# Merge gates of a hybrid encoder as seven products per block, with both branch projections ahead of them

## The reference, cut to what matters

```python
h = rms_norm(x, norm_g[layer])
z = h @ w_in[layer]
qa, ka, va, ga, qr, kr, vr, gr, gm = split_columns(z)
ya = (silu(ga) * attention(qa, ka, va)) @ w_branch_attn[layer]      # 512 -> 1024
yb = (silu(gr) * group_norm(retention(qr, kr, vr))) @ w_branch_ret[layer]   # 512 -> 1024
gates = sigmoid(gm).reshape(b, s, 2, d)                             # gm: 2048 columns of z
merged = gates[:, :, 0] * ya + gates[:, :, 1] * yb
x = x + merged @ w_out[layer]
```

## Time and profile before

| | |
|---|---|
| median of 3 runs | 1902.31 us |
| profiled execution | 1906.54 us |
| its span | 1904.7 us |
| TensorE matmuls | busy 1809.2 us, 95% of the span, x10784 |
| VectorE | busy 1062.2 us, 56% |
| ScalarE | busy 664.9 us, 35% |
| GpSimd | busy 696.1 us, 37% |
| DMA traffic | 96.09 MB, mean 50 GB/s |

### The profile page before, as it was taken

One profiled execution on the slowest core, in us unless ns is written; L12 is line 12 of the kernel. 1 busy time (PEld: TensorE's weight loads), 2 busy tenths in 40 slices (PEclk: granted clock), 3 DMA queues, 4 the chain that ended last, 5 costly groups with the idle time before them and its releaser, 6 DMA issues.

```text
span 1904.7 us, 30067 instructions
## 1 busy us (share of the span) xinstructions
PE 1809.2 (95%) x10784; PEld 1594.2 (84%) x10784; DVE 1062.2 (56%) x2378; ACT 664.9 (35%) x1551; POOL 696.1 (37%) x581
## 2 busy tenths in 40 slices
PE   6899989999999999999899998999999999999996
PEld 5788968899999888887687888889999988888875
...
DMA packets 129736, 96.09 MB, mean 50 GB/s; under 512 B 15712, under 2 KB 114272, under 8 KB 129632
## 3 DMA queue, kind: packets, MB, share of 16 engines
q1 hardware_dynamic: 127232, 89.42, 14.9%
...
## 4 chain that ended last, share of the span: by engine, by line
PE 74%; DVE 14%; POOL 4%; issue 4%; ACT 2%; DMA 1%; POOLq 0%; SPq 0%; DVEq 0%; ACTq 0%
PE ps L602 18%; PE ps L604 18%; PE ps L603 18%; PE ps L738 4%; PE ps L727 4%; DVE xh L1825 3%; PE ps L751 2%; PE ps L753 2%; POOL pp L483 2%; PE ps L844 2%; PE ps L828 1%; DVE lsum L1803 1%; DVE us L1678 1%; DVE hT_lo L1812 1%; PE ps L698 1%
## 5 line engine op out<-in xcount | busy, mean ns | idle before, releaser
L602 PE MATMUL ps<-w_hi,hT_hi 128*128 128x256 f32 (+1 forms) x1280 | 391.9, 306 | 12.8 <-DVE hT_lo L1436 4.9
L604 PE MATMUL ps<-w_hi,hT_lo 128*128 128x256 f32 (+1 forms) x1280 | 377.7, 295 | 0.0
L603 PE MATMUL ps<-w_lo,hT_hi 128*128 128x256 f32 (+1 forms) x1280 | 377.6, 295 | 0.0
L429 POOL TENSOR_SCALAR w_hi<-raw 128x1024 fp32r<-128x1024 f32 x97 | 102.8, 1060 | 558.2 <-PE ps L604 523.7
L602 PEld LDWEIGHTS ps<-w_hi,hT_hi 128*128 128x128 f32 x1280 | 245.7, 192 | 17.7 <-DVE hT_lo L1436 6.6
L602 PE MATMUL ps<-hT_hi,w_hi 128*128 128x512 f32 x640 | 255.2, 399 | 0.0
L604 PE MATMUL ps<-hT_hi,w_lo 128*128 128x512 f32 x640 | 252.2, 394 | 0.0
L603 PE MATMUL ps<-hT_lo,w_hi 128*128 128x512 f32 x640 | 252.0, 394 | 0.0
L603 PEld LDWEIGHTS ps<-w_lo,hT_hi 128*128 128x128 f32 x1280 | 245.9, 192 | 0.3
L604 PEld LDWEIGHTS ps<-w_hi,hT_lo 128*128 128x128 f32 x1280 | 245.5, 192 | 0.0
L483 POOL TENSOR_SCALAR pp<-pp,rrc 128x1024 f32<-128x1024 f32 x128 | 143.9, 1124 | 166.5 <-DVE rrc L1595 159.2
...
## 6 DMA issues: line engine op xcount, KB each, us to landing
raw<-w_in SPq DMA_DIRECT2D x167, 256.0 KB, 3.3
...
xh<-xs SPq DMA_DIRECT2D x8, 1024.0 KB, 9.6
raw<-w_a SPq DMA_DIRECT2D x16, 256.0 KB, 2.8
raw<-w_r SPq DMA_DIRECT2D x16, 256.0 KB, 3.2
w<-w_o SPq DMA_DIRECT2D x4, 1024.0 KB, 10.3
...
xh<-x SPq DMA_DIRECT2D x2, 1024.0 KB, 9.2
```

The lines of the kernel that those rows point to most:

```text
L429: nc.gpsimd.tensor_scalar(place(pos)[0], raw[:, slot], 1.0, 1.0, ALU.mult, ALU.mult).then_inc(w_rounded, 1)
L602: nc.tensor.matmul(outp, ah, bh, start=(start and i == 0), stop=False)
L603: nc.tensor.matmul(outp, ah, bl, start=False, stop=False)
L604: last = nc.tensor.matmul(outp, al, bh, start=False, stop=(stop and i == len(pairs) - 1))
```

## The change

The stage of gates and branches is rewritten, in both layers.

- Both branches come first: 16 groups of branch A, then 16 of branch B, 12 matmuls each, weights in 8 units of two blocks. ScalarE copies A's results to `y_st`, from which SyncE writes them to DRAM (`ys`); B's go to `xm`. The last head's crosses stand behind groups 0 and 1 of A, its turn-outs behind group 4.
- The gates of one block m are a 2 x 2 by 2 x 2 block product (token halves and channel halves of h; channel halves and kinds A/B of the weights), made as seven products of 12 matmuls each. VectorE makes four sums of quarters of h once per layer (`sum_3`, `sum_1`, `sum_2`, `sum_4`), which ScalarE and VectorE split into high and low parts; they lie in `ua_hi`, `ua_lo`, `ur_hi` and in place of a quarter of hT.
- Weights of the gates: GpSimd makes four sums or differences per block (`g_total`), ScalarE all seven high parts (`g_hi_part`), VectorE all seven low parts (`g_lo`). They run one block ahead, in eight slots.
- Product results: ScalarE copies the first (`g_first`), VectorE adds or subtracts the others (`give`) into four gate tiles in `w1x`; ScalarE takes tanh (`g_tanh`), VectorE merges with the branches (`merge_a` reads ya back from DRAM by way of `hb`, `merge_b`, `merge_sum`).
- The loops over m are written out, and the drain and wait on `phase_end` ahead of the stage are gone. The first O stage steps on VectorE and ScalarE stand between the additions of the last block, and SyncE's loads for the O stage hang on other events.

```diff
+N_Q = 7
+GIVES = ((((0, 0), None, 1),), (((0, 1), (0, 0), 1),), (((0, 0), (0, 0), 1),), (((1, 0), (0, 1), 1),),
+         (((1, 1), (1, 0), 1), ((0, 1), (0, 1), 1)), (((1, 0), (1, 0), -1),), (((0, 1), (0, 1), 1),))
+GIVEN = [0, 1, 2, 3, 5, 6, 7]
+N_GIVE = GIVEN[-1]
+TANHS = ((0, 0), (1, 1), (1, 0), (0, 1))
+HI_AT = (0, 2, 1, 3, 4, 5, 6)
+LO_DVE, LO_POOL = (0, 2, 1, 3, 4, 5, 6), ()
+N_S = 4
+E_OPS = 20
+E_DONE = {3: 6, 1: 12, 2: 16, 4: 20}
...
+        def g_slot(t_, x):
+            e = x % 8
+            return t_[:, 4 * (e % 2):4 * (e % 2) + 4, e // 2 * P:(e // 2 + 1) * P]
...
+                def spill(g):
+                    sp.wait_ge(y_ev, L * N_G + g + 1)
+                    sp.dma_start(ys[g // 2 * P:(g // 2 + 1) * P, g % 2 * 512:(g % 2 + 1) * 512], y_st[:, g % 2]).then_inc(y_out[g % 2], 16)
+                def gate_raw(m, b):
+                    mm = L * K + m
+                    if m:
+                        sp.wait_ge(*lo_done(mm - 1, (4, 3, 5, 6)[b]))
+                        if b == 0:
+                            sp.wait_ge(g_sum, 4 * mm)
+                    elif b < 2:
+                        sp.wait_ge(w_ready, 1 + u0 + U_A + K - 1 + b)
...
+                for v in range(6):
+                    branch_unit(v)
+                for g in range(N_G):
+                    spill(g)
+                    if g in (4, 9):
+                        branch_unit(6 + (g == 9))
+                for b in (0, 2, 1, 3):
+                    gate_raw(0, b)
+                y_back(0)
+                y_back(1)
...
-                sp.wait_ge(x_saved, L * 16 + 16)
-                sp.dma_start(w12[:], block(0, 1)).then_inc(o_w12a, 16)
-                sp.wait_ge(w_ready, 1 + L * U_L + U_L)
+                for m in range(1, K):
+                    for b in (1, 0, 2, 3):
+                        gate_raw(m, b)
+                    if m >= 2:
+                        y_back(m)
+                    if m == 1:
+                        sp.wait_ge(e_lo, (L + 1) * 2 * N_S)
+                        sp.dma_start(w12[:], block(0, 1)).then_inc(o_w12a, 16)
+                for q in (4, 6):
+                    sp.wait_ge(*lo_done((L + 1) * K - 1, q))
+                sp.wait_ge(g_sum, (L + 1) * K * 4)
                 sp.dma_start(w22, block(1, 1)).then_inc(o_w22, 16)
-                wait_apart(sp, d_ya, L * (2 * K) + 2 * K)
-                x_block(1, 1)
+                x7 = ((L + 1) * K - 1) * N_Q
+                sp.wait_ge(g_p, x7 + 2)
                 x_block(0, 1)
-                wait_apart(sp, d_yb, L * (2 * K) + 2 * K)
+                sp.wait_ge(d_mg, (L + 1) * N_G - 2)
                 for h in range(2):
                     sp.dma_start(w11[:, 2 * h:2 * h + 2], block(0, 0, 2 * h, 2)).then_inc(o_w11[h], 16)
+                sp.wait_ge(g_p, x7 + 4)
+                x_block(1, 1)
+                x_block(0, 0)
+                sp.wait_ge(d_mg, (L + 1) * N_G)
                 sp.dma_start(w11b, block(0, 1)).then_inc(o_w12, 16)
...
+                def fill_branch(v):
+                    if v >= 4:
+                        pool.wait_ge(d_ya, L * N_G + 4 * (v - 4) + 4)
+                    fill(v % 2, v % 4, L * PER[v % 2] + (3, 2)[v % 2] * KVH + 2 * RH + v // 2, n0 + U_A + v)
+                for v in range(2, K):
+                    fill_branch(v)
+                def g_free(m, q):
+                    x = m * N_Q + q
...
+                def g_total(m, n):
+                    mm = L * K + m
+                    x = mm * N_Q
+                    if n == 0:
+                        pool.wait_ge(g_in[1], 16 * (mm + 1))
+                        pool.wait_ge(*lo_done(mm, 0))
+                    elif n == 1:
+                        pool.wait_ge(g_in[3], 16 * (mm + 1))
+                        g_free(m, 1)
+                    elif n == 2:
+                        pool.wait_ge(*lo_done(mm, 2))
+                    if n:
+                        pool.wait_ge(g_sum, 4 * mm + n)
+                    out_, a, b = ((g_raw(0), g_raw(1), g_raw(0)), (g_slot(wsum, x + 1), g_raw(3), g_raw(0)),
+                                  (g_raw(2), g_slot(wsum, x + 1), g_raw(2)), (g_raw(1), g_raw(3), g_raw(1)))[n]
+                    nc.gpsimd.tensor_tensor(out_, a, b, ALU.subtract).then_inc(g_sum, 1)
+                for m in range(K):
+                    for n in range(4):
+                        g_total(m, n)
...
+                def branch(br, g):
+                    m, n = g // 2, g % 2
+                    if n == 0 and m % 2 == 0:
+                        pe.wait_ge(w_ready, 1 + L * U_L + U_A + 4 * br + m // 2 + 1)
+                    if g < 4:
+                        if br == 0:
...
+                        elif g == 0:
+                            pe.wait_ge(c_ul, (L + 1) * (RH * 2))
+                    else:
+                        pe.wait_ge((y_ev, r_ev)[br], L * N_G + g - 3)
+                    uh, ul = ((ua_hi, ua_lo), (ur_hi, ur_lo))[br]
+                    pos = m // 2
+                    prod3(ps[:, 4 * br + g % 4, :],
+                          [(w_u(4 * (m % 2) + k, pos * P, (pos + 1) * P),
+                            (uh[:, k, n * 512:(n + 1) * 512], ul[:, k, n * 512:(n + 1) * 512])) for k in range(KA)]
+                          ).then_inc((d_ya, d_yb)[br], 1)
                 update(RH - 1, T - 1)
...
+                for g in range(N_G):
+                    branch(0, g)
+                    if g < 2:
+                        cross(RH - 1, 2 * g)
+                        cross(RH - 1, 2 * g + 1)
+                    if g == 4:
+                        turn_out(RH - 1, 0)
+                        turn_out(RH - 1, 1)
+                for g in range(N_G):
+                    branch(1, g)
+                def gates(m, q):
+                    mm = L * K + m
+                    x = mm * N_Q + q
+                    pe.wait_ge(*lo_done(mm, q))
+                    if m == 0 and q in (1, 6):
+                        pe.wait_ge(e_lo, L * (2 * N_S) + (6 if q == 1 else 8))
+                    if m == 0 and q == 0:
+                        pe.wait_ge(y_ev, (L + 1) * N_G)
+                    if m == 0 and q >= 4:
+                        pe.wait_ge(r_ev, L * N_G + 12 + q - 3)
+                    elif x % (K * N_Q) == 7:
+                        pe.wait_ge(r_ev, (L + 1) * N_G)
+                    elif x % (K * N_Q) >= 8:
+                        if (x - 8) % N_Q == 0:
+                            pe.wait_ge(g_a, (x - 8) // N_Q + 1)
+                        else:
+                            pe.wait_ge(g_d, g_given(x - 8))
+                    wh, wl = g_slot(w_hi, x), g_slot(w_lo, x)
+                    prod3(ps[:, x % 8, :], [((wh[:, k], wl[:, k]), g_left(q, k)) for k in range(4)]).then_inc(g_p, 1)
+                for m in range(K):
+                    for q in range(N_Q):
+                        gates(m, q)
...
+                def spill(g):
+                    act.wait_ge(d_ya, L * N_G + g + 1)
+                    act.wait_ge(y_out[g % 2], 16 * (L * K + g // 2))
+                    nc.scalar.copy(y_st[:, g % 2], ps[:, g % 4]).then_inc(y_ev, 1)
...
+                def s_hi(n, at):
+                    for h in range(2):
+                        act.wait_ge(e_op, L * E_OPS + E_DONE[n] - 1 + h)
+                        nc.scalar.copy(s_split(n, h)[0], s_total(n, h)).then_inc(e_hi, 1)
+                def g_hi_part(m, q):
+                    mm = L * K + m
+                    x = m * N_Q + q
+                    if x < 8:
+                        act.wait_ge(d_yb, L * N_G + 4 * (x // 2) + 4)
+                    else:
+                        act.wait_ge(g_p, L * K * N_Q + x - 7)
+                    if q in (0, 2, 6):
+                        act.wait_ge(g_in[G_SRC[q]], 16 * (mm + 1))
+                    else:
+                        act.wait_ge(g_sum, 4 * mm + {4: 1, 1: 2, 5: 3, 3: 4}[q])
...
+                def g_first(m):
+                    mm = L * K + m
+                    act.wait_ge(g_p, mm * N_Q + 1)
+                    if m >= 2:
+                        act.wait_ge(d_mg, 2 * mm - 2)
+                    elif m == 0:
+                        act.wait_ge(d_yb, (L + 1) * N_G)
+                    nc.scalar.copy(gate_at(m, (0, 0)), ps[:, mm * N_Q % 8]).then_inc(g_a, 1)
+                def g_tanh(m, i):
+                    mm = L * K + m
+                    act.wait_ge(g_d, mm * N_GIVE + (2, 4, 6, 7)[i])
+                    o = gate_at(m, TANHS[i])
+                    nc.scalar.activation(o, o, ACT.Tanh, scale=0.5).then_inc(g_t, 1)
                 update(RH - 1, T - 1)
...
+                for g in range(N_G):
+                    spill(g)
+                    if g == 4:
+                        keep_out(RH - 1, 0)
+                        keep_out(RH - 1, 1)
+                for g in range(N_G):
+                    keep_y(g)
+                    if g == 3:
+                        s_hi(3, 0)
+                        g_hi_part(0, 0)
+                    elif g == 5:
```

(128 more changed lines are left out.)

281 lines of the change are left out of this document (147 added, 134 removed).

## The result

The kernel after takes 1878.70 us (median of 4 runs, 1877.16 to 1879.79), the kernel before 1902.78 beside it (1901.37 to 1903.28): a ratio of 0.988, interval 0.987 to 0.989. The forecast was 1884.0, range 1867 to 1903. The profiled execution took 1879.79, its span is 1878.0; before, 1906.54 and 1904.7.

The account below looks back on a forecast made before the run. TensorE's matmul count was taken to bound gates and branches, TensorE and VectorE together the O stage. Per layer -21.8 + 1.9 + 2.4 + 8.3 = -9.2, two layers -18.4, against the median 1902.31: 1884 us, range 1867 to 1903.

Parts of the forecast that it names:

- Matmuls: Gates: seven products of 12 matmuls instead of eight per block, 672 matmuls instead of 768: -21.8 us a layer.
- Pace: Gate products reading sums of h: 288 matmuls at 0.2333 us, not 0.2267: +1.9 us a layer, bounds 0 and 4.4.
- Start stalls: Branch A: crosses lose 0.4 us to the backward scan, turn-outs stall 2.0 (0 to 3.5): +2.4 us a layer.
- Branch B: VectorE's sums and splits of h take 47 us against 47.5 until product (0,1) wants them: cost nothing.
- Steady block: Gate blocks: VectorE 14.9, GpSimd 4.8, ScalarE 7.2 us, all under 19.2, so TensorE never waits: 19.2 us a block.
- Rival 3: Gate blocks: VectorE's in-order list, with GpSimd sums holding it, bounds them at 22 us a block: 1929 us; chance 0.2.
- Handover: Last gate block to O stage: VectorE starts 7.0 us later relative to TensorE, low clock +1.3: +8.3 a layer.
- rival 1: Handover costs 2 us a layer, no turn-out stall or slower pace: -19.8 a layer, about 1864 to 1876; chance 0.2.

Follow-up runs that it names:

- the two held fills: Kernel after with GpSimd's fill of branch unit 3 held until the backward scan ends and unit 4 until both halves' norm products are done: 1870.05 us, ratio 0.982.

## Why the prediction was right, and where it was not

1. **Matmuls, -21.8 a layer.** Right: 192 fewer in the whole, 96 x 0.2267 each layer.
2. **Pace, +1.9.** Wrong in sign. I put it on the tile as such; it was the tile's start, which the change moved. Instead of +1.9 there were -2.6 (384 branch matmuls at 0.2267, and the products of sums at 0.2267 too). The row had said "tile", and a line of the diff that I passed over said where the tile goes.
3. **Start stalls, +2.4.** The mechanism was right, the size a third: 7.1, by the two held fills. The turn-outs waited 2.74, inside my 0 to 3.5, but the scan was hit as well. I took its 2.97 us from the earlier trace rows, where GpSimd had been done by 604.45 (618.21 less its 13.76 idle), and gave it 0.4; now a fill runs through it. Low clock was not counted, and 1.7 to 1.9 of the 7.1 are that.
4. **Together** the stage was forecast at 251.4 and took 251.67 and 252.09. That is luck, for two errors cancelled: 4.5 too little gain in step 2, 4.7 too little loss in step 3.
5. **Branch B, cost 0.** Right: no wait of TensorE between 631 and 854 us. I had left the sums of h half a microsecond; the last split that product (0,1) waits for ends at 700.5, and the product starts at 705.16, so it was 4.7:

```profile
698.12 2.36 DVE L2038 TENSOR_TENSOR ua_hi<-xh,ua_hi 128x1024 fp32r<-128x1024 f32 x2
...
705.16 0.39 PE L754 MATMUL ps<-ua_hi,w_hi 128*128 128x512 f32 x1
```

6. **Steady block, 19.2.** Right, 19.04; one meeting with GpSimd of 0.56 (I had 0.7). Rival 3 was far off in these blocks, since VectorE could take 18.46. Its other half, that a late sum stops the in-order list, is real and nearer: 3.9 us of room, less than the 5.8 that VectorE is idle.
7. **Handover, +8.3.** Layer 1 shows it cleanly: 104.2 against 98.2, +6.0, within the bounds 2 and 11. The gap before product 1 is 4.40 and 4.21 (5.3 forecast), released by left_lo(1) as written; the low clock behind it was 0.50 and then 0.87 over two stretches of 5 us:

```profile
870.00:875.00 5.00, 4.79 (x11) 3.81 (x12) 5.00 (x3) 0.00 (x0) 5.00 (x2) 0.50 1.04 393
875.00:880.00 5.00, 5.00 (x21) 4.02 (x20) 5.00 (x6) 3.10 (x4) 0.70 (x1) 0.87 0.10 37
```

   0.50 is 1.2 GHz. The term that was too large is VectorE's late start, with the clock on top of it:

```profile
868.93 4.53 DVE L2155 TENSOR_TENSOR hT_lo<-lsum,hT_hi 128x1024 fp32r<-128x1024 f32 x2
873.39 4.53 DVE L2146 TENSOR_TENSOR lsum<-xm 128x1024 f32<-128x1024 f32 x2
```

   left_sum(3) ends 23.2 us behind the start of product 0, where it ended 17.0 behind it before (889.30 less 872.32): a shift of 6.2, not 7.0. The clash with GpSimd did not stay in size. It now holds left_lo(1) as well, for 2.2 us, and left_sum(3) for as much, 4.53 instead of the 6.75 before. And 6.2 is already as much as the +6.0, so low clock added nothing to VectorE's lateness, where I had added 1.3. In layer 0 the handover and all behind it cost 1.9 only, because the norm's chain came out in its short form, where the kernel before had the long one. I had given nothing to the norm between the layers.

The forecast missed the median by 5.3 us. In the span it is more, 26.7 us against 18.4, since the profiled execution of the kernel before lay 3.8 above its median. Of these 8.3, layer 0's handover and norm give 6.4, layer 1's handover 2.3, the stages -0.5. One sum of the prediction is off by itself: two layers of -19.8 bring rival 1 to 1862.7, not 1864.

The Trainium skill, "SBUF — State Buffer", section "Who interferes with whom", has the lock between VectorE and GpSimd; these traces agree, and put a price on it: 4.4 us for one sum of 4.8 beside four low parts, nothing beside additions with one operand in PSUM.
